# Spreading the rows of cumulated decays over the partitions: matmuls, or transfers through DRAM

## The reference, cut to what matters

```python
def ssd_chunked(xh, dt, a, bm, cm):
    ...
    a_cum = jnp.cumsum(a_dt, axis=-1)
    causal = jnp.tril(jnp.ones((SSD_CHUNK, SSD_CHUNK), dtype=bool))
    decay = jnp.exp(jnp.where(causal, a_cum[..., :, None] - a_cum[..., None, :], -jnp.inf))
    cb = jnp.einsum("bclgn,bcsgn->bgcls", cc, bc)
    y_diag = jnp.einsum("bgecls,bcsgep->bclgep", cb[:, :, None] * decay, x)
    ...
```

## Time and profile before

| | us |
|---|---|
| median of 3 runs | 1659.84 |
| lowest, highest | 1659.65, 1662.24 |
| the profiled execution | 1662.67 |
| its span, first to last instruction | 1660.7 |
| granted clock of TensorE, mean (share of full) | 0.989 |
| busy: TensorE, VectorE, ScalarE, GpSimd | 1578.0, 1036.5, 856.5, 74.1 |

### The profile page before, as it was taken

The page is one execution under the profiler, slowest core; times in us unless marked ns, Lnnn a source line. Parts: engine busy times, 40 slices in busy tenths (PEclk is TensorE's granted clock), DMA queues, the critical chain, the costliest instruction groups (busy, mean ns, idle before and its releaser), DMA issues.

```text
span 1660.7 us, 21594 instructions
## 1 busy us (share of the span) xinstructions
PE 1578.0 (95%) x8022; PEld 1329.3 (80%) x8022; DVE 1036.5 (62%) x1313; ACT 856.5 (52%) x1004; POOL 74.1 (4%) x38
## 2 busy tenths in 40 slices
PE   5999999999999999999999999999999799889987
PEld 5888888788778887988888788778888688668876
DVE  5978875555664544778885655564553665666664
ACT  4556666454354444556666554354443555554463
POOL 0011111000000000011111000000000010001000
PEclk9999999999999999999999999999999899989999
DMA  6444444344455464444444434445545452436251
GB/s 225 153 153 149 136 150 167 134 152 152 151 189 194 158 206 150 178 152 152 140 141 170 147 139 152 152 162 210 193 166 221 171 181 102 156 123 231 101 186 47
DMA packets 40114, 265.47 MB, mean 160 GB/s; under 512 B 4407, under 2 KB 5592, under 8 KB 9560
## 3 DMA queue, kind: packets, MB, share of 16 engines
q1 hardware_dynamic: 37816, 259.89, 43.8%
q10 hardware_dynamic: 2208, 4.35, 0.7%
HBM read 262.39 MB, written 1.84 MB: 159 GB/s over the span
## 4 chain that ended last, share of the span: by engine, by line
PE 78%; DVE 8%; issue 6%; ACT 6%; DMA 1%; ACTq 0%; DVEq 0%; SPq 0%
PE ps L563 21%; PE ps L565 20%; PE ps L564 20%; PE ps L568 4%; ACT w_high L1067 3%; PE ps L841 2%; DVE scratch L1461 2%; PE ps L842 2%; PE ps L843 2%; DVE w_low L1461 2%; PE ps L695 2%; DVE conv L1554 1%; ACT w_high L1289 1%; PE ps L729 1%; DMA h<-in_x 1%
## 5 line engine op out<-in xcount | busy, mean ns | idle before, releaser
L1461 DVE TENSOR_TENSOR w_low<-w_raw,w_high 128x2048 fp32r<-128x2048 f32 (+2 forms) x252 | 567.3, 2255 | 485.2 <-ACT w_high L1067 407.3
L1067 ACT ACTIVATE w_high<-w_raw 128x2048 fp32r<-128x2048 f32 (+1 forms) x198 | 372.6, 1883 | 379.8 <-PE ps L565 359.1
L563 PE MATMUL ps<-w_high,u_high 128*128 128x512 f32 x1376 | 552.1, 401 | 13.2 <-DVE w_low L1461 8.5
L565 PE MATMUL ps<-w_high,u_low 128*128 128x512 f32 x1376 | 538.8, 392 | 0.0
L564 PE MATMUL ps<-w_low,u_high 128*128 128x512 f32 x1376 | 538.0, 391 | 0.0
L563 PEld LDWEIGHTS ps<-w_high,u_high 128*128 128x128 f32 x1376 | 260.0, 189 | 70.2 <-issue 7.5
L565 PEld LDWEIGHTS ps<-w_high,u_low 128*128 128x128 f32 x1376 | 259.5, 189 | 56.1
L564 PEld LDWEIGHTS ps<-w_low,u_high 128*128 128x128 f32 x1376 | 260.1, 189 | 52.8 <-issue 1.9
L563 PE MATMUL ps<-w_high,b_high 128*128 128x512 f32 x384 | 152.5, 397 | 1.9 <-issue 1.9
L565 PE MATMUL ps<-w_high,b_low 128*128 128x512 f32 x384 | 149.8, 390 | 0.0
L564 PE MATMUL ps<-w_low,b_high 128*128 128x512 f32 x384 | 149.5, 389 | 0.0
(11 more groups left out here) (238 smaller groups left out, 1453.0 us busy)
## 6 DMA issues: line engine op xcount, KB each, us to landing
w_raw<-in_stream SPq DMA_DIRECT2D x238, 1024.0 KB, 4.8
w_raw<-in_stream SPq DMA_DIRECT2D x10, 512.0 KB, 3.4
par<-in_pars SPq DMA_DIRECT2D x4, 265.0 KB, 5.0
ple_gain<-in_ple_g ACTq DMA_DIRECT2D x2, 512.0 KB, 6.1
scratch<-rev ACTq DMA_DIRECT2D x2, 512.0 KB, 8.3
w_raw<-in_stream SPq DMA_DIRECT2D x4, 256.0 KB, 2.5
out<-h SPq DMA_DIRECT2D x2, 512.0 KB, 2.6
scratch<-in_const SPq DMA_DIRECT2D x1, 768.0 KB, 6.9
```

Of the source, the lines that this page charges most:

```text
L563: nc.tensor.matmul(o, hi, whi, start=start, stop=False, **kw)
L565: return nc.tensor.matmul(o, lo, whi, start=False, stop=stop, **kw)
L1067: nc.scalar.activation(WH[:, c % RING, 0:n], W[:, c % RING, 0:n], ACT.Copy).then_inc(high_ready, 1)
L1461: return nc.vector.tensor_tensor(out=o, in0=a, in1=b, op=op)
```

## The change

The row a_cum[l] no longer goes over TensorE. ScalarE stores the turned decays (64 rows of 128) to a small DRAM array `rows_dram`, and issues, per group and token half, a load that repeats the group's 8 rows on all 128 partitions, straight into `ssd_decay` (512 KB each). GpSimd adds the mask to it in place (`mask_rows`, in place of `rows_of`), and the exponentials run in place, from SBUF. TensorE's four matmuls per group and half go. The first half's exponentials move from 2i+7 to 2i+8, in the stream behind the state copy; the state product no longer waits for them. The turned decays are no longer split in high and low.

GpSimd's stream becomes: for each g `mask_rows(g, 0)`, `state_input(g)`, `mask_rows(g, 1)`, `gate(g)`.

```diff
@@ TensorE
-                    turn(ps[:, 5, 0:P], cum_hl[:, :, :].rearrange("p t n -> p (t n)").bitcast(F32)).then_inc(cumt_ps.sem, 1)
+                    turn(ps[:, 5, 0:P], acum).then_inc(cumt_ps.sem, 1)
...
-                    for t, at_c in ((0, 2 * i + 6), (1, 2 * i + 8)):
-                        if c == at_c:
-
-                            if t == 1:
-                                pe.wait_ge(state_out.sem, state_out.at(l, g + 1))
-                            elif g == 0:
-                                pe.wait_ge(cb_masked.sem, cb_masked.at(l, 1))
-                            else:
-                                pe.wait_ge(ssd_y.sem, ssd_y.at(l, 2 * g))
-                                pe.wait_ge(qk_out.sem, qk_out.at(l, g))
-
-                            pe.wait_ge(decay_rows.sem, decay_rows.at(l, g + 1))
-                            one_col = (tri_r, later_r)[t][:, P // 2 - 1:P // 2].to_broadcast([P, P])
-                            for b in range(2):
-                                nc.tensor.matmul(four(ps[:, 6 + b, :]), ident_r[:, :], bc(never_r[:, :].unsqueeze(1), 4, P),
-                                                 start=True, stop=False)
-                                last = nc.tensor.matmul(ps[:, 6 + b, :], one_col, DR[:, b * 512:(b + 1) * 512],
-                                                        start=False, stop=True)
-                            last.then_inc(row_ps.sem, 1)
                     if c == 2 * i + 7:
                         pe.wait_ge(xds_ready.sem, xds_ready.at(l, g + 1))
-                        pe.wait_ge(ssd_exp.sem, ssd_exp.at(l, 2 * g + 1))
+                        if g:
+                            pe.wait_ge(state_out.sem, state_out.at(l, g))
+                            pe.wait_ge(qk_out.sem, qk_out.at(l, g))
+                        else:
+                            pe.wait_ge(cb_masked.sem, cb_masked.at(l, 1))
...
                     if c == 2 * i + 10:
-                        pe.wait_ge(ssd_exp.sem, ssd_exp.at(l, 2 * g + 2))
+                        pe.wait_ge(state_out.sem, state_out.at(l, g + 1))
+                        if g:
+                            pe.wait_ge(qk_out.sem, qk_out.at(l, g))
@@ ScalarE
+            def load_rows(l, g, t):
+                if g:
+                    act.wait_ge(yd_ps.sem, yd_ps.at(l, 2 * (g - 1) + t + 1))
+                act.dma_start(EM[t], bass.AP(rows_dram.tensor, (t * HEADS + g * HPG) * P, [[0, P], [P, HPG], [1, P]]))\
+                    .then_inc(row_loaded[t], 16)
...
                         nc.scalar.activation(cumT, ps[:, 5, 0:P], ACT.Copy).then_inc(cumt_out.sem, 1)
+                        act.wait_ge(cumt_out.sem, cumt_out.at(l, 1))
+                        act.dma_start(rows_dram, cumT[0:T * HEADS, :]).then_inc(rows_stored, 16)
+                    if c == 11:
+                        act.wait_ge(rows_stored, (l + 1) * 16)
+                        load_rows(l, 0, 0)
+                        load_rows(l, 0, 1)
+                    for g, i in enumerate(XT[:-1]):
+                        for t in range(T):
+                            if c == 2 * i + 11 + t:
+                                load_rows(l, g + 1, t)
...
-                        for t, at_c in ((0, 2 * i + 7), (1, 2 * i + 9)):
+                        for t, at_c in ((0, 2 * i + 8), (1, 2 * i + 9)):
                             if c == at_c:
-                                act.wait_ge(row_ps.sem, row_ps.at(l, 2 * g + t + 1))
-                                if g:
-                                    act.wait_ge(yd_ps.sem, yd_ps.at(l, 2 * (g - 1) + t + 1))
+                                act.wait_ge(row_masked.sem, row_masked.at(l, 2 * g + t + 1))
                                 for e in range(HPG):
                                     a = t * HEADS + g * HPG + e
-                                    ins = nc.scalar.activation(EM[t][:, e, :], ps[:, 6 + e // 4, tok(e % 4)], ACT.Exp,
+                                    ins = nc.scalar.activation(EM[t][:, e, :], EM[t][:, e, :], ACT.Exp,
                                                                bias=nacum[:, a:a + 1])
@@ GpSimd
-            nc.gpsimd.tensor_copy(ident_r[:, :], ident)
-            nc.gpsimd.tensor_scalar(never_r[:, :], later, NEG, None, ALU.mult)
+            nc.gpsimd.tensor_scalar(never[:, :], later, NEG, None, ALU.mult)
...
-                rows_of(0)
+                def mask_rows(g, t):
+                    pool.wait_ge(row_loaded[t], l * (16 * GROUPS) + 16 * (g + 1))
+                    nc.gpsimd.tensor_tensor(out=EM[t], in0=EM[t],
+                                            in1=bc(never[:, :].unsqueeze(1), HPG, P), op=ALU.add).then_inc(row_masked.sem, 1)
+
                 for g in range(GROUPS):
+                    mask_rows(g, 0)
                     state_input(g)
-                    if g < GROUPS - 1:
-                        rows_of(g + 1)
+                    mask_rows(g, 1)
                     gate(g)
@@ VectorE
-                        nc.vector.tensor_copy(acum, ps[:, 5, 0:3 * HEADS])
-                        chain.then(dve, nc.vector.tensor_copy(cum_hl[:, :, 0:HEADS], two(ps[:, 5, 0:T * HEADS])))
-                        tt(cum_hl[:, :, HEADS:2 * HEADS], two(ps[:, 5, 0:T * HEADS]), cum_hl[:, :, 0:HEADS].bitcast(F32), ALU.subtract)\
-                            .then_inc(cum_out.sem, 1)
+                        nc.vector.tensor_copy(acum[:, 0:3 * HEADS], ps[:, 5, 0:3 * HEADS]).then_inc(cum_out.sem, 1)
```

More of the change, by code:

```diff
@@ L99 @@
 K_KDEC = K_ROPE1 + 2 * T * 32
-K_HEAD = K_KDEC + 4
-N_CONST1 = K_HEAD + HEADS
+N_CONST1 = K_KDEC + 4
 K_ROPE2 = 0
@@ L105 @@
 N_CONST2 = K_QPOW + 4 * P
-VCH1, SCH1 = 75, 4
+VCH1, SCH1 = 74, 4
 VCH2, SCH2 = 23, 5
@@ L139, in bc, with build @@
     return ap.to_broadcast([P, *shape])
-def build(nc, stream1, stream2, pars, const1, const2, onehot, relb, final_g, ple_g, w_x, out, rev):
+def build(nc, stream1, stream2, pars, const1, const2, onehot, relb, final_g, ple_g, w_x, out, rev, rows_dram):
     ctx = ExitStack()
@@ L302, in build @@
         adt = tiny(T * HEADS)
-        acum = tiny(3 * HEADS)
+        acum = tiny(4 * HEADS)
         nacum = tiny(T * HEADS)
@@ L475, in build @@
         rev_stored = sem("rev_stored")
+        rows_stored = sem("rows_stored")
+        row_loaded = [sem(f"row_loaded{t}") for t in range(T)]
         stored = sem("stored")
@@ L2061 @@
     rev = nc.dram_tensor("rev", (P, 4 * REV), F32, kind="Internal").ap()
+    rows_dram = nc.dram_tensor("rows", (T * HEADS, P), F32, kind="Internal").ap()
     args["w_x"] = args.pop("x")
-    build(nc, out=out, rev=rev, **args)
+    build(nc, out=out, rev=rev, rows_dram=rows_dram, **args)
     r = run_bass_kernel_spmd(nc, [{f"in_{n}": a for n, a in arrays.items()}], core_ids=[0])
```

18 lines of the change are left out of this document (3 added, 15 removed).

## The result

The changed kernel takes 1682.63 us (median of 4 executions, 1679.24 to 1685.00), the kernel before beside it 1659.74. The ratio is 1.0122, with a 95% interval of 1.0108 to 1.0136: 22.9 us slower. The direction was forecast, the size was not: 1668 was said, with a range that ended at 1677. The profiled execution took 1685.0 us around a span of 1683.0.

A forecast was written before the change was run, and what follows sets the result against it. TensorE was taken as the bound, with VectorE's chain close behind. Per layer -7.4 (matmuls) +0.2 (first turns) +5.2 (turns) +6.1 (state products) = +4.1, twice +8.2: 1668 us, range 1657 to 1677.

The forecast's parts named there:

- The work removed: TensorE's 16 batches of four matmuls on the decay rows go: 0.92 us each, 14.7 us, 7.4 per layer.
- The wait at the turns: TensorE waits some 2.6 us for VectorE's adds at the turns of groups 2 and 3: 5.2 per layer.
- the table load lies on this chain: ScalarE's exponential table load, 1.28 us, stands between state copy and exponentials, after the state product starts.
- group 1's turns are spared: No new wait there: group 0's exponentials already wait 4.28 us for TensorE, which absorbs the moved ones.
- The wait at the state product: TensorE waits for GpSimd's state input, behind mask and w_low: 2.1 us for group 2, 6.1 a layer together.
- My doubt about the scales: Whether VectorE's two y scalings wait for GpSimd's mask: taken as 0.9 us; without it 3.4 a layer, not 6.1.
- The transfers: Store and row loads hidden, taken as 0; group 0 covered by 3 us, +4 kept for the range.
- The first turns: ScalarE's decay copy and store precede the B columns' copy; with two VectorE operations removed, +0.2 us a layer, -0.4 to +0.6.
- the rivals with fewer waits: TensorE stays the bound, no waits, 1645 us, chance 0.13; VectorE's chain shorter than added, 1657 to 1665, chance 0.17.
- The shorter chain: Rival: the chain after the state product is shorter, turns wait 2.6 per layer; 1657 to 1665 us, chance 0.17.
- the larger mask: Bound at the state products: GpSimd's mask add takes 2.3 us instead of 2.0, giving 7.1 a layer.

The follow-up runs named there:

- the runs without waits: Fastest version 1645.44 us; the same with seven row loads per layer doubled 1644.23; changed kernel without mask adds, first-half exponentials back at 2i+7, 1645.44.
- run 2: Changed kernel with a tiny exponential added on ScalarE, so the table load comes ahead of the state copy: 1673.96 us, ratio 1.0076.
- the second execution: Changed kernel profiled again, unaltered, in a second series: median 1678.92 us, ratio 1.0113.
- the fastest version: Changed kernel with state input before mask, table load earlier, xdt product first, second-half exponentials at 2i+10, ScalarE's copies before the k0 tile: 1645.44 us, ratio 0.9899.
- run 8: Fastest version with three idle VectorE additions ahead of the y adds of groups 1 and 2, making TensorE wait: 1660.88 us, ratio 1.0000.
- run 3: Changed kernel with matmuls of zeros filling TensorE's new waits: 1685.49 us with fillers behind the convolution wait, 1680.18 with them ahead of it.
- the two series: Changed kernel measured twice, unaltered, beside the kernel before: 1682.63 us (22.9 slower) and 1678.92 us (17.2 slower).

## Why the prediction was right, and where it failed

- **The work removed** was right: 0.92 per batch, 14.7 us. It comes out whole in the runs without waits.
- **The wait at the turns** was right in place, cause and size: 2.6 said, 3.06 measured. The chain from the state product to the end of the adds is 31.5 us (142.16 to 173.69), where 31.0 was said. The two batches of exponentials on it account for that: from the start of one to the split behind it the rows give 2.36 and 2.34 us in place of 2.01. I had kept those at zero in the sum and at most 0.5 per period in the bounds. That the table load lies on this chain (run 2) and that group 1's turns are spared were right too.
- **The wait at the state product** was right in its mechanism: scales behind the mask, then w_low ahead of the state input. Said were 1.7, 2.1 and 2.3 for groups 1 to 3; the rows give 1.73 and 2.12 for groups 1 and 3 of the first layer. For group 2 they give 0.14, where the stretch at 175 us had made TensorE late, and 1.81 in the second execution, which has no stretch there. My doubt about the scales is settled: 1.88 for two, where 0.89 was the price alone. By the Trainium skill ("SBUF — State Buffer", "Who interferes with whom") a tensor_scalar in a two-port mode takes the lock, and the trace agrees. The mask's 2.37 instead of 2.0 is just over the 2.3 of my bounds and under the 2.40 of the rows; behind w_low it ends at 182.53, 8.8 us after the adds (which end at 173.69), where 8.6 was said.
- **The transfers** were taken as 0 in the sum, with 3 us of cover for group 0. The cover was used up: the store took 5.0 us where I said 2, and the state input was there at 99.5 us where I said near 96 (the terms that I gave add up to 94.9). In the changed kernel's two profiles this makes 0.20 and 2.05 us of waits at group 0's state products, in a sum of 23. For groups 1 to 3 the loads were hidden, as said. In the fastest version, where the store is issued 1.8 us earlier and lands in 1.8, group 0 has no wait, and doubling the loads cost nothing there. It was not run in the changed kernel.
- **The first turns** waited 0.75 a layer longer (2.0 against 1.25), where +0.2 was said with +0.6 as the bound. The store, 0.5 us of ScalarE's time, and the wait for the copy stand ahead of the copy of the B columns.
- Together the waits make -14.7 + 22.9 = **+8.2, against the +8.2 forecast.** That the match is this close is luck in part, as the terms were off by up to 2.5 us in both directions: at the state products 12.2 were said and 9.7 measured, at the turns 10.4 and 11.7.
- **The step that failed is one that was not there.** The sum takes each microsecond that TensorE waits as one microsecond. The prediction quotes a granted clock of 1.00 in the stage, uses it to say that TensorE is the bound, and then drops it. The change gives TensorE eleven gaps of 1.7 to 3.1 us in a stage whose longest was 1.35, and at five or six of them it then ran at half speed for 3.4 us. With the stretches at old waits that is seven to nine, in place of two: 13.7 us in the profiled execution, 8.6 in the next, and 11.0 on average over all executions. With this term the forecast would have stood near 1679 (1668 + 11); and the rivals with fewer waits should have carried less of it.
- **One sum of the prediction is wrong.** The shorter chain, with 3.4 to 6.1 at the state products, gives -1.2 to +1.5 us per layer, up to 1663, and not +2.5 and 1665; that would need the 7.1 of the larger mask. The forecast does not hang on it.

That waits bring these stretches was argued from the trace first, and two runs bear on it from either side: waits put into a kernel that had none raise them from 10.2 to 23.9 us, all of it at the new waits (run 8), and waits filled with useless matmuls take those at new waits from five or six to none (run 3). Since their number differs between executions of one kernel, single profiles carry this only together: the seven profiles without fillers that have 8 us or more of new waits show 3.4 to 20.5 us of stretches at them, the three with less show none. What stays open is why one wait is followed by a stretch and the next of the same length is not, and the exact share of the clock in the 17.2 and 22.9 us of the two series; 11 us is the average over both.

## What to carry to other kernels

When work is taken from an engine that has no gap, ask what its clock rests on. Each new stall of 2 to 3 us in this kernel's TensorE cost up to another 1.7 us by the clock, and about 1 us on average (11.0 us for eleven stalls), so a change that exchanges matmuls for waits of the same length loses here. And the order of three streams was worth more than the change itself: 14.7 us of matmuls became 17 to 23 us slower or 16 us faster, depending on which of two ready operations stood first in GpSimd's, ScalarE's and VectorE's streams. Before a change is given up, take its new waits one by one, find what starts the chain of each, and move that.

## What had not been expected of the hardware

- The granted clock was 0.51 over 3.41 us right behind a wait of 3.06 us (175.01:178.42), with TensorE busy throughout; it is back at 1.00 afterwards. The matmuls' distance is 0.43 us in it, 0.23 outside.
- The places of such stretches move between executions of the same kernel. The kernels with stalls also spread wider: 11 us over 5 executions of the changed kernel and 10 over 11 of the one that was made to wait, against 1 over 4 of the fastest one. But the kernel before spreads by 5.6 over its 40, so few executions show too little of it.
- Eight exponentials of 128x128 take 2.45 us when they read SBUF in place and 2.17 when they read PSUM.
- A stretch at half clock ahead of a wait is partly free: at group 2's state product the changed kernel shows a wait of 0.14, and the one without the stretch 1.57 us.
